# Inverses of two delta rules: half of the heads' Y on the other half of the partitions, products in all four quarters, updates of half the columns

## The chip, the cores and the metric

The kernel runs on one core of a Trainium2 chip, as one program. The metric is the time of one execution on the device in microseconds (us), of which a median of several runs is given. TensorE multiplies, VectorE and ScalarE work on its results in PSUM and on SBUF, GpSimd on SBUF alone, and the DMA queues move data. Each engine runs its own instructions in order; semaphores hold them together.

## What is computed

Two transformer blocks over 1024 tokens of width 1024, one after the other. Each has a mixer with a delta rule. The first block's has 6 heads and two directions, in chunks of 64 tokens:

```python
kb = k * beta[..., None]
a = jnp.where(strict, jnp.einsum('bhnld,bhnsd->bhnls', kb, k) * lmask, 0.0)
t = lax.linalg.triangular_solve(a + eye, jnp.broadcast_to(eye, a.shape),
                                left_side=True, lower=True, unit_diagonal=True)
u = jnp.einsum('bhnls,bhnse->bhnle', t, v * beta[..., None])
wk = jnp.einsum('bhnls,bhnsd->bhnld', t, kb * jnp.exp(gc)[..., None])
```

The second block's has 8 heads and one direction. The reference writes it as a scan over the tokens; the kernel works in chunks of 64 as well and needs the same kind of inverse:

```python
sa = jnp.einsum('bhvk,bhk->bhv', st, a_t)
st = st * w_t[:, :, None, :] + sa[..., None] * b_t[:, :, None, :] + v_t[..., None] * k_t[:, :, None, :]
```

The inverse of each 64x64 triangular matrix is what the change is about. Projections, attention and feed-forward layers take the rest.

## The kernel before

**Units.** 128 tokens are two chunks; chunk c lies on partitions 64c to 64c+63. A unit is the two chunks of all heads of one direction: 16 units of 12 blocks in the first block (`gdn`), 8 units of 16 blocks in the second (`b2`). A block is 64 partitions by 64 columns, block (c, h) at columns 64h. Everything here is float32.

**The inverse.** With M the strict triangle, X starts as the unit matrix minus M's first off-diagonal, and five levels (`LEVELS`, block sizes b = 2, 4, 8, 16, 32) each join pairs of blocks of size b. The kernel holds X both ways round, Xt (turned) and Xa. A level is: Y = the product of M and Xt (`gd_y`, `rw_y`), masked by VectorE to the part that level b fills (lines 1636 and 2950, into Ym); then the products of Xa and Ym (`gd_xt`, `rw_xt`) and of Ym and Xa (`gd_xa`, `rw_xa`); then VectorE subtracts the first from Xt (lines 1642, 2955) and the second from Xa (1644, 2957). The last level makes no Xa. All these products go through `pe_blocks` (matmul at lines 1551 and 2682), which goes through the heads and for each through c = 0 and 1: rows 0 to 63 of the array with output partitions 0 to 63, then rows 64 to 127 with 64 to 127. Ahead of the levels, `gd_t` and `rw_t` (lines 1584, 2885) turn the start by a product with the unit matrix; VectorE adds the unit matrix to give Xt (1632, 2945), and GpSimd adds it to the unturned start for Xa (1687, 2986).

**Other products of 64x64 blocks.** The key products (line 1576, and `pe_features`, line 2695), those of the state (1720, 1734, 3011) and w (1605, 2919) change their row half and output half with every product.

**Order.** Every engine's function is a generator; `together` and `loop` step through them in the same order on every engine. In the first block interval n steps the scan of an earlier pair of units, the second half of unit n-1 and the first half of unit n, and between them the neighbourhood attention (`pe_na` and its companions). In the second, interval i steps the scan of unit i-2 (`pe_scan`), the inverse of unit i-1 (`pe_in`), the preparation of unit i (`pe_pre`) and, at half the pace, the attention `pe_fox`, whose rest follows the loop.

**Banks.** PSUM has 8 banks. `bk.take(key, ring)` gives the next bank of a ring; `bk.pair` is a bank and the one after it. `bk.room` waits until the last holder has been emptied. In the first block `PAIR` is bank 0 (with 1) for kk, w and the scan's products, `ONE_BANK` the ring 2, 3, 4 for everything else. In the second, `PAIR` is bank 0 (with 1) and `ONE_BANK` the ring 2, 3. Attention has its own.

## Time and profile before

| | us |
|---|---|
| median of 3 runs | 4546.52 |
| lowest, highest | 4536.28, 4548.52 |
| the profiled execution | 4550.43 |
| its span | 4549.1 |
| first block's delta rule with neighbourhood attention | 658 to 1071 |
| second block's delta rule with attention | 2761 to about 3334, then attention alone |

The profile is one execution. Busy time counts the time in which an engine has an instruction in work; matmul records overlap, so their durations add up to more. A float32 product of 64x64 blocks appears as two records. PE is the matmul, PEld the weight load, DVE is VectorE, ACT ScalarE, POOL GpSimd; L1551 is a line of the kernel. In the groups, "busy, mean ns | idle before" ends with what ended the idle time.

### The profile page before, as it was taken

To read this page: it belongs to the slowest core of one execution; us is meant where nothing else is said; L and a number is where in the kernel's file an instruction comes from. 1 tells how busy PE (TensorE), PEld (TensorE's weight loads), DVE (VectorE), ACT (ScalarE), POOL (GpSimd) and SP (SyncE) were. 2 spreads that over 40 slices of the span, in tenths; PEclk is the share of its full clock that TensorE was granted. 3 is DMA by queue.
4 is the path that set the end of the run, shared out by engine and by line. 5 is a ranking of instruction groups with operands and counts; after the bars stand their busy time and mean duration, and the time that the engine had idled before them with its cause. 6 is when DMAs were issued, how large, how long until landed. Compare 5 with 4: busy or idle time off the path is not lost. (4 is left out here: it accounts for less than half of the span.)

```text
span 4549.1 us, 75162 instructions
## 1 busy us (share of the span) xinstructions
PE 4046.0 (89%) x33230; PEld 3288.3 (72%) x33230; DVE 2075.1 (46%) x3302; ACT 1251.5 (28%) x1786; POOL 454.3 (10%) x442
## 2 busy tenths in 40 slices
PE   6999849995898899999899996878868989999979
PEld 5788727774676688888588785666656768888867
DVE  4633426554333444445513214655633365655662
ACT  4222244332222221121411214334221232222231
POOL 0001102231201000000200002232201200000010
PEclk9999869997899899999899998998967989999989
DMA  5211120113112111111122323011003211111101
GB/s 180 87 43 62 45 74 6 30 30 139 40 37 93 38 55 47 47 47 55 65 95 89 116 88 90 26 52 44 7 33 137 97 41 52 47 47 47 56 31 63
DMA packets 213687, 281.94 MB, mean 62 GB/s; under 512 B 15580, under 2 KB 170972, under 8 KB 213236
## 3 DMA queue, kind: packets, MB, share of 16 engines
q1 hardware_dynamic: 176048, 185.58, 13.0%
q10 hardware_dynamic: 37316, 91.56, 5.3%
q8 instruction: 263, 4.31, 0.4%
q14 instruction: 60, 0.49, 0.0%
HBM read 217.11 MB, written 60.00 MB: 61 GB/s over the span
## 5 line engine op out<-in xcount | busy, mean ns | idle before, releaser
L425 PE MATMUL ps<-sb_a_h,sb_whi 128*128 128x512 f32 (+1 forms) x3008 | 1206.1, 401 | 128.5 <-DVE sb_a_h L516 66.2
L426 PE MATMUL ps<-sb_a_h,sb_wlo 128*128 128x512 f32 (+1 forms) x3008 | 1192.3, 396 | 0.0
L427 PE MATMUL ps<-sb_a_h,sb_whi 128*128 128x512 f32 (+1 forms) x3008 | 1191.7, 396 | 0.0
L425 PEld LDWEIGHTS ps<-sb_a_h,sb_whi 128*128 128x128 f32 (+1 forms) x3008 | 575.4, 191 | 289.5 <-issue 91.4
L427 PEld LDWEIGHTS ps<-sb_a_h,sb_whi 128*128 128x128 f32 (+1 forms) x3008 | 576.7, 192 | 123.7
L426 PEld LDWEIGHTS ps<-sb_a_h,sb_wlo 128*128 128x128 f32 (+1 forms) x3008 | 578.1, 192 | 118.6 <-issue 1.0
L387 DVE TENSOR_TENSOR sb_wlo<-sb_wraw,sb_whi 128x2048 fp32r<-128x2048 f32 (+3 forms) x146 | 315.8, 2163 | 428.7 <-ACT sb_whi L379 405.0
L1850 DVE TENSOR_TENSOR sb_x<-sb_x,ps 128x512 f32<-128x512 f32 x480 | 314.4, 684 | 299.3 <-PE ps L427 299.1
L379 ACT ACTIVATE sb_whi<-sb_wraw 128x2048 fp32r<-128x2048 f32 (+3 forms) x146 | 260.4, 1784 | 678.1 <-PE ps L427 509.1
L425 PE MATMUL ps<-sb_a_g,sb_whi 128*128 128x512 f32 x896 | 349.7, 390 | 9.6 <-DVE sb_x L1850 9.6
L426 PE MATMUL ps<-sb_a_g,sb_wlo 128*128 128x512 f32 x896 | 348.6, 389 | 0.0
L427 PE MATMUL ps<-sb_a_g,sb_whi 128*128 128x512 f32 x896 | 348.6, 389 | 0.0
L479 POOL TENSOR_TENSOR sb_squares<-sb_squares,sb_a_f 128x512 f32<-128x512 f32 x70 | 88.4, 1275 | 1847.4 <-ACT sb_a_f L471 1846.9
L1551 PEld LDWEIGHTS ps<-sb_b 64*64 64x64 f32 x5760 | 184.6, 136 | 57.7 <-issue 23.6
L1551 PE MATMUL ps<-sb_b 64*64 64x64 f32 x5760 | 200.2, 221 | 21.5 <-DVE sb_b L1644 10.5
L425 PEld LDWEIGHTS ps<-sb_a_g,sb_whi 128*128 128x128 f32 x896 | 168.2, 188 | 48.4 <-DVE sb_x L1850 13.8
L427 PEld LDWEIGHTS ps<-sb_a_g,sb_whi 128*128 128x128 f32 x896 | 168.2, 188 | 35.1
L426 PEld LDWEIGHTS ps<-sb_a_g,sb_wlo 128*128 128x128 f32 x896 | 168.2, 188 | 34.7
L2682 PEld LDWEIGHTS ps<-sb_b 64*64 64x64 f32 x3840 | 133.6, 148 | 64.1 <-DVE sb_b L2957 19.4
L2682 PE MATMUL ps<-sb_b 64*64 64x64 f32 x3840 | 147.2, 234 | 32.1 <-DVE sb_b L2957 11.6
L2096 DVE TENSOR_TENSOR sb_a_f<-sb_a_f 128x512 f32<-128x512 f32 x64 | 44.3, 692 | 185.3 <-ACT sb_a_f L2122 185.3
L513 DVE SCALAR_TENSOR_TENSOR sb_a_f<-sb_x,sb_params,sb_a_f 128x1024 f32<-128x1024 f32 x48 | 83.5, 1763 | 32.2 <-PEq L335 25.0
(467 smaller groups left out, 4980.5 us busy)
## 6 DMA issues: line engine op xcount, KB each, us to landing
sb_wraw<-w_in SPq DMA_DIRECT2D x33, 1024.0 KB, 5.4
sb_wraw<-w_ff SPq DMA_DIRECT2D x32, 1024.0 KB, 5.2
sb_wraw<-w_up SPq DMA_DIRECT2D x22, 1024.0 KB, 5.1
sb_wraw<-w_down SPq DMA_DIRECT2D x11, 1024.0 KB, 4.9
sb_wraw<-w_xkv SPq DMA_DIRECT2D x8, 1024.0 KB, 5.7
sb_wraw<-w_out SPq DMA_DIRECT2D x8, 1024.0 KB, 5.1
sb_a_f<-y ACTq DMA_DIRECT2D x16, 512.0 KB, 5.3
gates<-sb_a_f ACTq DMA_DIRECT2D x32, 256.0 KB, 2.0
```

The lines of the kernel that those rows point to most:

```text
L379: e.activation(WH[j % 2][:, 0:m], WR[j % 2][:, 0:m], ACT.Copy).then_inc(s_whi, 1)
L387: e.tensor_tensor(WL[j % 2][:, 0:m], WR[j % 2][:, 0:m], WH[j % 2][:, 0:m].bitcast(F32), ALU.subtract).then_inc(s_wlo, 1)
L425: e.matmul(o, wh[:, k, c], xh[:, sl], start=(k == 0), stop=False)
L426: e.matmul(o, wl[:, k, c], xh[:, sl], start=False, stop=False)
L427: m = e.matmul(o, wh[:, k, c], xl[:, sl], start=False, stop=(k == t.nk - 1))
L479: e.tensor_tensor(ACC[n % 2], ACC[n % 2], bufs[n % len(bufs)], ALU.add).then_inc(*sa.up())
L513: e.scalar_tensor_tensor(b, xk(k), gain(k), rstd, ALU.mult, ALU.mult).then_inc(*rn.up())
L1551: m = e.matmul(block(ps, c, h), block(lhs, c, h), block(rhs, c, h), start=True, stop=True)
L1850: e.tensor_tensor(o, o, bk[t.key], ALU.add).then_inc(*bk.empty(t.key))
L2096: e.tensor_tensor(b, b, b, ALU.mult).then_inc(*ff_sq.up())
L2682: m = e.matmul(block(ps, c, h), block(lhs, c, h), block(rhs, c, h), start=True, stop=True)
```

## The change

The heads are split into two halves (g = 0 and 1: heads 0 to 2 and 3 to 5, or 0 to 3 and 4 to 7). For the second half Y and Xa lie on the other half of the partitions: the Y of chunk c is written to partitions of chunk 1-c. `quarters()` goes through the products so that successive ones take different quarters of the array; each half of the heads writes a bank of its own, so Y, X and t take pairs, and the first block's rings become pairs 0 and 2 and the single bank 4. Since a level changes only every second run of b columns of X, the products of Xt and Xa stream those 32 columns only (`second`), and VectorE subtracts 192 or 256 columns, not 384 or 512. The Xt and Xa products share one pair (`gd_x`, `rw_x`); the Xa products keep the order of `blocks()`, with outputs in the pair's first bank. The start of Xa for the second half of the heads comes from six (eight) more products with the unit matrix as weights and one more sum on VectorE; GpSimd's sum covers only the first half. The diff, with the second block's part cut to its changed lines (its Y and X products are as in the first, with 4 for 3 heads, 128 for 96 and 256 for 192 columns, `odd` fixed at 1, and its rings unchanged):

```diff
@@ -1514,7 +1514,7 @@
-            PAIR, ONE_BANK = (0,), (2, 3, 4)
+            PAIR, ONE_BANK = (0, 2), (4,)
...
+            def second(ap, b, odd):
+                return ap.rearrange("p (n z b) -> p n z b", z=2, b=b)[:, :, odd]
+
+            def quarter(ps, c, g, q, w):
+                return ps[64 * c:64 * c + 64, g, w * q:w * q + w]
+
+            def small(ap, c, h):
+                return ap[64 * c:64 * c + 64, 32 * h:32 * h + 32]
+
+            def quarters():
+                return [(c, g, q) for q in range(3) for c in range(2) for g in range(2)]
...
-                ps = bk.take(("gd_t", n), ONE_BANK)
+                bk.take(("gd_t", n), PAIR)
+                ps = bk.pair(("gd_t", n))
                 e.wait_ge(*gd_x0[d].at(s))
                 e.wait_ge(*bk.room(("gd_t", n)))
                 for c, h in blocks():
-                    m = e.matmul(block(ps, c, h), block(Xt, c, h), C("eye", 64 * c, 64 * c + 64), start=True, stop=True)
+                    e.matmul(block(ps[:, 0], c, h), block(Xt, c, h), C("eye", 64 * c, 64 * c + 64), start=True, stop=True)
+                for q in range(3):
+                    for c in range(2):
+                        m = e.matmul(block(ps[:, 1], 1 - c, q), C("eye", 64 * c, 64 * c + 64), block(Xt, c, 3 + q), start=True, stop=True)
                 m.then_inc(*bk.fill(("gd_t", n)))
                 yield
-                for lv in range(5):
-                    e.wait_ge(*bk.emptied(("gd_xa", n, lv - 1) if lv else ("gd_t", n)))
-                    pe_blocks(e, ("gd_y", n, lv), ONE_BANK, M, Xt)
+                odd = 1 - d
+                for lv, b in enumerate(LEVELS):
+                    e.wait_ge(*bk.emptied(("gd_x", n, lv - 1) if lv else ("gd_t", n)))
+                    if lv == 0:
+                        e.wait_ge(*gd_xa0[d].at(s))
+                    bk.take(("gd_y", n, lv), PAIR)
+                    ps = bk.pair(("gd_y", n, lv))
+                    e.wait_ge(*bk.room(("gd_y", n, lv)))
+                    for c, g, q in quarters():
+                        m = e.matmul(quarter(ps, 1 - c if g else c, g, q, 64), block(M, c, 3 * g + q), block(Xt, c, 3 * g + q),
+                                     start=True, stop=True)
+                    m.then_inc(*bk.fill(("gd_y", n, lv)))
                     yield
                     e.wait_ge(*bk.emptied(("gd_y", n, lv)))
-                    pe_blocks(e, ("gd_xt", n, lv), ONE_BANK, Xa, Ym)
+                    bk.take(("gd_x", n, lv), PAIR)
+                    ps = bk.pair(("gd_x", n, lv))
+                    e.wait_ge(*bk.room(("gd_x", n, lv)))
+                    for c, g, q in quarters():
+                        o = 1 - c if g else c
+                        m = e.matmul(v3(quarter(ps, c, g, q, 32), b), block(Xa, o, 3 * g + q),
+                                     second(block(Ym, o, 3 * g + q), b, odd), start=True, stop=True)
                     if lv < 4:
-                        pe_blocks(e, ("gd_xa", n, lv), ONE_BANK, Ym, Xa)
-                    yield
-                e.wait_ge(*bk.emptied(("gd_xt", n, 4)))
+                        for c, h in blocks():
+                            m = e.matmul(v3(small(ps[:, 0, 96:288], c, h), b), block(Ym, c, h),
+                                         second(block(Xa, c, h), b, 1 - odd), start=True, stop=True)
+                    m.then_inc(*bk.fill(("gd_x", n, lv)))
+                    yield
+                e.wait_ge(*bk.emptied(("gd_x", n, 4)))
                 e.wait_ge(*gd_kbv.at(n))
                 pe_blocks(e, ("gd_u", n), ONE_BANK, Xt, R(vbs[d], 384))
                 bk.take(("gd_w", n), PAIR)
...
+                pair = bk.pair(("gd_t", n))
                 e.wait_ge(*bk.filled(("gd_t", n)))
                 e.wait_ge(*gd_xa0[d].at(s))
-                e.tensor_tensor(v6(Xt), v6(bk["gd_t", n][:, 0:384]), m6("eye"), ALU.add).then_inc(*bk.empty(("gd_t", n)))
-                yield
+                e.tensor_tensor(v6(Xt), v6(pair[:, 0, 0:384]), m6("eye"), ALU.add).then_inc(*vo.up())
+                e.tensor_tensor(v6(Xa[:, 192:384]), v6(pair[:, 1, 0:192]), b3(C("eye"), 3, 64), ALU.add).then_inc(*bk.empty(("gd_t", n)))
+                yield
+                odd = 1 - d
                 for lv, b in enumerate(LEVELS):
                     e.wait_ge(*bk.filled(("gd_y", n, lv)))
-                    e.tensor_tensor(v6(Ym), v6(bk["gd_y", n, lv][:, 0:384]), m6(f"L{b}" if d else f"LT{b}"),
+                    e.tensor_tensor(gq(Yms[d]), bk.pair(("gd_y", n, lv))[:, :, 0:192].rearrange("p g (q e) -> p g q e", q=3),
+                                    C(f"L{b}" if d else f"LT{b}").unsqueeze(1).unsqueeze(1).to_broadcast([128, 2, 3, 64]),
                                     ALU.mult).then_inc(*bk.empty(("gd_y", n, lv)))
                     yield
-                    e.wait_ge(*bk.filled(("gd_xt", n, lv)))
+                    pair = bk.pair(("gd_x", n, lv))
+                    x = Xt.rearrange("p (g n z b) -> p g n z b", g=2, z=2, b=b)[:, :, :, odd]
+                    e.wait_ge(*bk.filled(("gd_x", n, lv)))
+                    e.tensor_tensor(x, x, pair[:, :, 0:96].rearrange("p g (n b) -> p g n b", b=b),
+                                    ALU.subtract).then_inc(*(vo.up() if lv < 4 else bk.empty(("gd_x", n, lv))))
                     if lv < 4:
-                        e.wait_ge(*bk.filled(("gd_xa", n, lv)))
-                    e.tensor_tensor(Xt, Xt, bk["gd_xt", n, lv][:, 0:384], ALU.subtract).then_inc(*bk.empty(("gd_xt", n, lv)))
-                    if lv < 4:
-                        e.tensor_tensor(Xa, Xa, bk["gd_xa", n, lv][:, 0:384], ALU.subtract).then_inc(*bk.empty(("gd_xa", n, lv)))
+                        x = second(Xa, b, 1 - odd)
+                        e.tensor_tensor(x, x, v3(pair[:, 0, 96:288], b), ALU.subtract).then_inc(*bk.empty(("gd_x", n, lv)))
                     yield
...
                 e.wait_ge(*gd_x0[d].at(s))
-                e.tensor_tensor(v6(R(Xas[d], 384)), m6("eye"), v6(R(Xts[d], 384)), ALU.add).then_inc(*gd_xa0[d].up())
+                e.tensor_tensor(v6(R(Xas[d], 192)), b3(C("eye"), 3, 64), v6(R(Xts[d], 192)), ALU.add).then_inc(*gd_xa0[d].up())
...
@@ -2878,11 +2936,15 @@
-                ps = bk.take(("rw_t", i), ONE_BANK)
+                bk.take(("rw_t", i), PAIR)
+                ps = bk.pair(("rw_t", i))
-                    m = e.matmul(block(ps, c, h), block(R(XT, 512), c, h), C("eye", 64 * c, 64 * c + 64), start=True, stop=True)
+                    e.matmul(block(ps[:, 0], c, h), block(R(XT, 512), c, h), C("eye", 64 * c, 64 * c + 64), start=True, stop=True)
+                for q in range(4):
+                    for c in range(2):
+                        m = e.matmul(block(ps[:, 1], 1 - c, q), C("eye", 64 * c, 64 * c + 64), block(R(XT, 512), c, 4 + q), start=True, stop=True)
...
@@ -2940,21 +3019,25 @@
+                pair = bk.pair(("rw_t", i))
-                e.tensor_tensor(v6(R(XT, 512)), v6(bk["rw_t", i]), m8("eye"), ALU.add).then_inc(*bk.empty(("rw_t", i)))
+                e.tensor_tensor(v6(R(XT, 512)), v6(pair[:, 0]), m8("eye"), ALU.add).then_inc(*vo.up())
+                e.tensor_tensor(v6(R(XA + 256, 256)), v6(pair[:, 1, 0:256]), b3(C("eye"), 4, 64), ALU.add).then_inc(*bk.empty(("rw_t", i)))
-                    e.tensor_tensor(v6(R(Y, 512)), v6(bk["rw_y", i, lv]), m8(f"LT{b}"), ALU.mult).then_inc(*bk.empty(("rw_y", i, lv)))
-                    yield
-                    e.wait_ge(*bk.filled(("rw_xt", i, lv)))
+                    e.tensor_tensor(gq(R(Y, 512)), split(bk.pair(("rw_y", i, lv)), 0), m24(f"LT{b}"), ALU.mult).then_inc(*bk.empty(("rw_y", i, lv)))
+                    yield
+                    pair = bk.pair(("rw_x", i, lv))
+                    x = R(XT, 512).rearrange("p (g n z b) -> p g n z b", g=2, z=2, b=b)[:, :, :, 1]
+                    e.wait_ge(*bk.filled(("rw_x", i, lv)))
+                    e.tensor_tensor(x, x, pair[:, :, 0:128].rearrange("p g (n b) -> p g n b", b=b),
+                                    ALU.subtract).then_inc(*(vo.up() if lv < 4 else bk.empty(("rw_x", i, lv))))
-                        e.wait_ge(*bk.filled(("rw_xa", i, lv)))
-                    e.tensor_tensor(R(XT, 512), R(XT, 512), bk["rw_xt", i, lv], ALU.subtract).then_inc(*bk.empty(("rw_xt", i, lv)))
-                    if lv < 4:
-                        e.tensor_tensor(R(XA, 512), R(XA, 512), bk["rw_xa", i, lv], ALU.subtract).then_inc(*bk.empty(("rw_xa", i, lv)))
+                        x = second(R(XA, 512), b, 0)
+                        e.tensor_tensor(x, x, v3(pair[:, 0, 128:384], b), ALU.subtract).then_inc(*bk.empty(("rw_x", i, lv)))
```

## Rows read from the trace of the kernel before

**Rows 1.** The page's first part: busy time and share of the span
```profile
PE 4046.0 (89%) x33230; PEld 3288.3 (72%) x33230; DVE 2075.1 (46%) x3302; ACT 1251.5 (28%) x1786; POOL 454.3 (10%) x442
```

**Rows 2.** Busy time by stretch, both delta-rule stages; PEclk is granted clock
```profile
658.00:1071.00 413.00, 369.62 (x10380) 312.45 (x10380) 234.09 (x526) 149.13 (x305) 118.63 (x136) 0.98 0.10 26
2750.00:3330.00 580.00, 449.37 (x8288) 367.07 (x8286) 333.26 (x709) 209.27 (x346) 146.03 (x152) 0.90 0.16 46
```

**Rows 3.** Groups by line, first delta-rule stage: busy, mean | idle before
```profile
L1551 PE MATMUL ps<-sb_b 64*64 64x64 f32 x5760 | 200.2, 221 | 21.5 <-DVE sb_b L1644 10.5 <-issue 5.2 <-DVE sb_b L1636 3.4
...
L1642 DVE TENSOR_TENSOR sb_b<-sb_b,ps 128x384 f32<-128x384 f32 x80 | 44.3, 553 | 68.8 <-PE ps L1551 68.1
L1644 DVE TENSOR_TENSOR sb_b<-sb_b,ps 128x384 f32<-128x384 f32 x64 | 35.0, 547 | 0.0
```

**Rows 4.** Order of time, one level of the first unit, alone
```profile
675.10 0.92 PE L1551 MATMUL ps<-sb_b 64*64 64x64 f32 x24 [1.19 <-DVE sb_b L1644]
...
676.67 1.61 PE L1551 MATMUL ps<-sb_b 64*64 64x64 f32 x48 [0.66 <-DVE sb_b L1636]
...
679.48 0.74 PE L1551 MATMUL ps<-sb_b 64*64 64x64 f32 x18 [1.19 <-DVE sb_b L1644]
```

**Rows 5.** Groups by line, second delta-rule stage
```profile
L2682 PE MATMUL ps<-sb_b 64*64 64x64 f32 x3840 | 147.2, 234 | 32.1 <-DVE sb_b L2957 11.6 <-DVE sb_b L2950 9.4 <-DVE sb_b L3099 6.5
...
L2955 DVE TENSOR_TENSOR sb_b<-sb_b,ps 128x512 f32<-128x512 f32 x40 | 27.5, 686 | 57.0 <-PE ps L2682 56.7
...
L2957 DVE TENSOR_TENSOR sb_b<-sb_b,ps 128x512 f32<-128x512 f32 x32 | 21.8, 680 | 0.0
...
L2776 DVE TENSOR_TENSOR sb_b<-sb_b 128x512 f32<-128x512 f32 x8 | 11.2, 1405 | 0.3
...
L3073 DVE TENSOR_TENSOR sb_b<-sb_b,ps 128x256 f32<-128x256 f32 x16 | 6.7, 419 | 12.3 <-PE ps L3027 12.3
```

**Rows 6.** Order of time, second stage: two-quarter and four-quarter products
```profile
3261.28 1.16 PE L2695 MATMUL ps<-sb_b 64*64 64x64 f32 x64
...
3292.34 2.08 PE L2682 MATMUL ps<-sb_b 64*64 64x64 f32 x64
```

**Rows 7.** Order of time, first stage's end: four-quarter product
```profile
1069.04 0.58 PE L1734 MATMUL ps<-sb_x,sb_b 64*64 64x64 f32 x24 [1.25 <-DVE sb_x L1758]
```

**Rows 8.** Order of time, second stage: full-array weights, 64 and 128 columns
```profile
2945.23 1.95 PE L2390 MATMUL ps<-sb_x 128*128 128x64 f32 x16
...
2961.63 1.12 PE L3055 MATMUL ps<-sb_b 128*128 128x128 f32 x8
```

**Rows 9.** Waits, first stage: us in total, times, longest
```profile
PEld ps L1551 <- DVE sb_b L1644: 20.3, 25, 1.4
...
PEld ps L1551 <- DVE sb_b L1636: 9.2, 18, 0.9
```

**Rows 10.** Waits, second stage
```profile
PEld ps L2682 <- DVE sb_b L2957: 19.4, 18, 1.6
...
PEld ps L2682 <- DVE sb_b L2950: 16.4, 17, 2.4
```

**Rows 11.** Line 2682: its engine idle before it until (us, times)
```profile
  DVE sb_b L3099: 13.5, 8
```

**Rows 12.** Order of time, second stage: state product, then the transposing product
```profile
3263.94 1.15 PE L3011 MATMUL ps<-sb_b 64*64 64x64 f32 x32 [1.50 <-DVE sb_b L2941]
...
3265.74 0.69 DVE L3069 TENSOR_TENSOR sb_b<-sb_b,ps 64x512 f32<-64x512 f32 x1
...
3266.08 1.15 PE L2885 MATMUL ps<-sb_consts,sb_b 64*64 64x64 f32 x32
```

**Rows 13.** Busy time by stretch inside the second stage
```profile
2800.00:2850.00 50.00, 38.28 (x826) 30.53 (x825) 29.37 (x65) 17.69 (x35) 16.94 (x19) 0.97 0.12 30
...
3000.00:3050.00 50.00, 37.89 (x554) 29.90 (x554) 27.35 (x63) 17.84 (x34) 15.33 (x15) 0.83 0.08 23
...
3300.00:3350.00 50.00, 28.51 (x392) 22.74 (x386) 16.64 (x28) 17.14 (x20) 2.71 (x4) 0.77 0.20 68
```

More of the change, by code:

```diff
@@ L1652, in ac_prep @@
                 if n >= 2:
-                    e.wait_ge(*bk.emptied(("gd_xt", n - 2, 4)))
+                    e.wait_ge(*bk.emptied(("gd_x", n - 2, 4)))
                 if s >= 2:
@@ L2675, in block, with second, quarter, small @@
                 return ap[64 * c:64 * c + 64, 64 * h:64 * h + 64]
+            def second(ap, b, odd):
+                return ap.rearrange("p (n z b) -> p n z b", z=2, b=b)[:, :, odd]
+            def quarter(ps, c, g, q, w):
+                return ps[64 * c:64 * c + 64, g, w * q:w * q + w]
+            def small(ap, c, h):
+                return ap[64 * c:64 * c + 64, 32 * h:32 * h + 32]
+            def quarters():
+                return [(c, g, q) for q in range(4) for c in range(2) for g in range(2)]
             def pe_blocks(e, key, lhs, rhs):
@@ L2898, in pe_in @@
                     yield
-                for lv in range(5):
-                    e.wait_ge(*bk.emptied(("rw_xa", i, lv - 1) if lv else ("rw_t", i)))
-                    pe_blocks(e, ("rw_y", i, lv), R(M, 512), R(XT, 512))
+                for lv, b in enumerate(LEVELS):
+                    e.wait_ge(*bk.emptied(("rw_x", i, lv - 1) if lv else ("rw_t", i)))
+                    if lv == 0:
+                        e.wait_ge(*rw_xa0.at(i))
+                    bk.take(("rw_y", i, lv), PAIR)
+                    ps = bk.pair(("rw_y", i, lv))
+                    e.wait_ge(*bk.room(("rw_y", i, lv)))
+                    for c, g, q in quarters():
+                        m = e.matmul(quarter(ps, 1 - c if g else c, g, q, 64), block(R(M, 512), c, 4 * g + q),
+                                     block(R(XT, 512), c, 4 * g + q), start=True, stop=True)
+                    m.then_inc(*bk.fill(("rw_y", i, lv)))
                     yield
                     e.wait_ge(*bk.emptied(("rw_y", i, lv)))
-                    pe_blocks(e, ("rw_xt", i, lv), R(XA, 512), R(Y, 512))
+                    bk.take(("rw_x", i, lv), PAIR)
+                    ps = bk.pair(("rw_x", i, lv))
+                    e.wait_ge(*bk.room(("rw_x", i, lv)))
+                    for c, g, q in quarters():
+                        o = 1 - c if g else c
+                        m = e.matmul(v3(quarter(ps, c, g, q, 32), b), block(R(XA, 512), o, 4 * g + q),
+                                     second(block(R(Y, 512), o, 4 * g + q), b, 1), start=True, stop=True)
                     if lv < 4:
-                        pe_blocks(e, ("rw_xa", i, lv), R(Y, 512), R(XA, 512))
+                        for c, h in blocks():
+                            m = e.matmul(v3(small(ps[:, 0, 128:384], c, h), b), block(R(Y, 512), c, h),
+                                         second(block(R(XA, 512), c, h), b, 0), start=True, stop=True)
+                    m.then_inc(*bk.fill(("rw_x", i, lv)))
                     yield
-                e.wait_ge(*bk.emptied(("rw_xt", i, 4)))
+                e.wait_ge(*bk.emptied(("rw_x", i, 4)))
                 e.wait_ge(*bk.emptied(("rw_g", i)))
```

2 lines of the change are left out of this document (1 added, 1 removed).

## The prediction

> **What bounds the kernel now.** I read the page's first part, then busy time by stretch, then the groups and waits of the two stages, then the order of time. The page says that TensorE is busy for 89% of the span and VectorE for 46% [rows 1]. The change touches only two stages: the first block's delta rule (413 us) and the second block's (580 us, of which the last part is attention alone). In the first TensorE is busy 369.6 us of 413 (0.895), in the second 449.4 of 580 (0.775); VectorE has 234 and 333 us [rows 2]. So nothing outside these 993 us can move, and inside them TensorE comes first.
>
> Busy TensorE is not all of it. The inverses are a ping-pong: a product of TensorE, an update of VectorE, a product. The order of time shows one level of the first unit with nothing beside it: the Y product starts at 675.10, the products of Xt and Xa take 1.61 us from 676.67, and the next level's Y product starts at 679.48, released by the update of line 1644, 4.38 us after the last [rows 4]. In the steady state other units, attention and the scan fill the gaps: the idle time of the matmuls of line 1551 is 21.5 us in all, and of line 2682 it is 32.1 [rows 3, 5]. The weight loads, which start first, wait for the update of Xa (lines 1644 and 2957) 25 times for 20.3 us, and 18 times for 19.4 us [rows 9, 10]. So I take TensorE's issue as the bound for most of both stages, and VectorE's updates as a part of the path where those waits stand.
>
> **TensorE, what is saved.** A float32 product of 64x64 blocks is two records (5760 records for the first stage's 16 units of 180 products). All products of a level now go in a diagonal order: two quarters of the array. For 64 such records the trace has 2.08 us; taking 0.22 us as the length of a single record (mean 221 ns, rows 3), (2.08 - 0.22)/63 = 29.5 ns a record. The products of line 2695 change their quarter with every product and use all four: 64 records take 1.16 us, 14.9 ns a record [rows 3, 6]. The first stage has the same pair: 48 records in 1.61 us, 29.6 ns, against 24 in 0.58 us, 15.7 ns [rows 4, 7]. So four quarters halve the spacing, by 14.6 ns a record. The changed Y and Xt products use all four.
>
> First stage, a unit: 5 Y batches and 5 Xt batches of 24 records, 240 x 14.6 ns = 3.5 us saved. The turned Xa of the second half of the heads comes from 6 more products (12 records, two quarters, 0.35 us). Net 3.15 us, times 16 units = 50.4 us. Second stage, a unit: 10 batches of 32 records, 4.67 us, less 16 records more, 0.47 us: 4.2 us, times 8 = 33.6 us.
>
> **Half the columns.** Xt's and Xa's products now stream 32 columns, not 64. No row shows a product of 32. The nearest is the step from 128 to 64 columns with weights of 128 columns: 8 records of 128 columns take 1.12 us (140 ns each with the tail), 16 records of 64 columns 1.95 us (122 ns each) [rows 8]. Half the columns gave 13%, not half. The weights keep their 64 columns in this change, and I take the same to hold: nothing gained. The bounds are no gain and half the spacing; half would save 5 x 24 x 7.5 ns + 4 x 24 x 14.8 ns = 2.3 us a unit in the first stage and 3.1 in the second, with the shares of use below 33 + 19 = 52 us.
>
> The Trainium skill, TensorE: Matmul & The Clock Gate, section LDWEIGHTS (loading the stationary operand), states that a load takes its columns over 1.2 GHz whatever its rows; by that rule a 64-column load is an estimated 53 ns in each quarter, and a narrower stream behind it gains nothing. The trace agrees: full-array records of 64 columns are spaced 122 ns or less, near the load of 128 columns that the rule puts at 107.
>
> **VectorE.** 512 columns take 686 ns and 256 take 419 [rows 5]: 1.04 ns a column. In the first stage each update loses 192 of 384 columns, 0.20 us; nine a unit make 1.80, and the added sum with the unit matrix on the other half costs 0.547 - 0.20 = 0.35 us. That is 1.45 x 16 = 23 us of busy time. In the second stage 9 x 0.267 - 0.42 = 1.98 us, times 8 = 16 us. Only what TensorE waits for counts: 25 waits x 0.40 us (two updates) = 10 and 18 x 0.53 = 9.6 us [rows 9, 10], less the added sum at the same shares of use (16 x 0.35 x 25/64 + 8 x 0.42 x 18/32 = 4.1 us). That is 15.5 us. The Y mask keeps its 384 or 512 columns. Its wait is the smaller one (9.2 and 16.4 us) and stays.
>
> The updates now touch runs of 2, 4, 8, 16 and 32 columns. No row has such runs. Lower bound: no cost. Upper bound: the slowest float32 rate in the stage, 1405 ns for 512 columns, 2.74 ns a column [rows 5]; then 192 columns take 0.67 and 256 take 0.85 us, and the updates get 0.12 and 0.17 us longer instead of shorter. I take no cost, since what slows that row is no property that its shape shows, and 686 ns is the rate of every update out of PSUM here.
>
> The Trainium skill, Vector Engine (DVE) Microarchitecture Reference, section 5.2 Measured stream behaviour on trn2, states that runs of two adjacent aligned words stream at the full rate; by it the sum stands as it is. No run here shows it yet.
>
> **How much of TensorE's saving arrives.** In slices where TensorE waits anyway, shorter products only lengthen the wait. I take the busy shares of the stages: 50.4 x 0.895 = 45.1 and 33.6 x 0.775 = 26.0, together 71.1 us.
>
> **Waits that move.** In the first stage the rings change from one pair and three banks to two pairs and one bank. A fill waits for the fill two before it. Following the order, those are nearly always the unit's own dependence (Y before X before Y); the key product kk and the scan's second product wait for less. The lone bank holds only decays, u and outputs, each emptied some rounds before. I count nothing, covered by that distance; without it each of about 16 intervals would pay one VectorE step of 0.55 us, 9 us. In the second stage t, Y and X leave banks 2 and 3 for the only pair, which the state product uses. There t now waits until VectorE has emptied that product: the second of its two operations starts at 3265.74 and ends at 3266.43, while t issues at 3266.08 [rows 12]. That is 0.4 us where an attention step stands between them, up to 1.4 where none does (the product starts at 3263.94 and lasts 1.15); behind t queue the g and kv products and VectorE's masks. 7 units x 1.0 = 7 us lost. Against it, products no longer wait for banks that output work holds: 13.5 us of idle in 8 waits on line 3099 [rows 11], of which I take half, since the same VectorE operation still stands ahead of the consumer in its queue. The two cancel. GpSimd's sum is halved and its end was not the last thing waited for; TensorE's new wait for it is met already by VectorE's. Nothing.
>
> **Sum.** 71.1 + 15.5 = 87 us. The profiled execution took 4550.4 us (span 4549.1), 3.9 above the median of 4546.5. 4550.4 - 87 = 4463.8, less 3.9: **4460 us**, 1.9% faster.
>
> **Rivals.**
> Narrow products do run in half the time. For it: 140 to 122 ns is for full-width weights, and quarter products are only bounded together. Against it: the 13%. It gives 4460 - 52 = 4408. Chance 0.12.
> Short runs slow VectorE to the upper bound: 43 waits get 0.25 to 0.33 us longer where I had them shorter, 12 us lost for 20 gained: 4492. Chance 0.08.
> Four quarters do not overlap. In the rows of four quarters each row half of the array writes a bank of its own; in the change both row halves write into each bank, on different partitions. Then only the 9 us of added products and VectorE's 15.5 us are left: about 4540, within 0.3%. Against it: the diagonal order also puts both halves in one bank, and each quarter's spacing is the same there (2 x 29.5) as with four (4 x 14.9). Chance 0.05.
> The Trainium skill, TensorEngine Tiling (Array Packing), section Gotcha 1: PSUM Pressure, says that different row tiles cannot access the same PSUM bank simultaneously; this is the rule that speaks for that rival. The two-quarter rows speak against it as far as different partitions go.
> The clock decides, and the kernel is slower. With less work between the same waits TensorE's granted clock may fall (a mean over its two levels, 2.4 GHz as 1.00 and 1.2 GHz as 0.50). It is 0.98 and 0.90 over the two stages [rows 2], and inside the second 0.97 where TensorE is busy 38.28 of 50 us, but 0.83 at 37.89 and 0.77 at 28.51 [rows 13]. At 0.83 in both stages the cost is 369.6 x (0.98/0.83 - 1) + 449.4 x (0.90/0.83 - 1) = 67 + 38 = 105 us, more than the 87: 4550.4 + 18 - 3.9 = 4565 us, slower by 0.4%. It decides from a granted clock of 0.846 in both; at that point gain and loss are equal. Against it: four quarters at once keep the array at least as full while it works, and the first stage stands near 1.00. Chance 0.05.
> That the saving is mostly off the path (half arrives): 4503. Chance 0.07.
>
> **How the numbers follow.** The forecast's own case has 0.63, with 4435 to 4485 for the choice of shares. The range 4400 to 4525 takes in the narrow, the short-run and the half case and leaves out the bank and the clock case and small tails. A change under 0.3% (14 us) can't be told from none. Faster by more: 0.90; within: 0.05; slower: 0.05.
>
> **What would show it.** In the profile after: 24 records of the Y product in about 0.58 us and 32 in 0.70, the X products (48) in about 1.27 us and (64) in 1.65, updates of 192 columns at 0.35 us and of 256 at 0.42, the first unit's level at about 3.3 us from 4.38, TensorE busy some 50 and 34 us less, clocks near 0.98 and 0.90. X products of 0.8 us would mean that narrow ones are cheap; Y products still at 0.92 that the quarters don't overlap; updates of 0.55 that runs cost. New waits of t for line 3069 above 1.5 us, or of X for another unit's bank, would make me wrong from the other side.

## The result and the profile after

The changed kernel took 4516.12 us in the median of five runs (4504.9 to 4522.52) beside 4548.17 us for the kernel before on the same chip: ratio 0.9929 [0.9907, 0.995], 32 us saved. The forecast was 87 us (4460), so the direction was right, and the time lies inside the range of 4400 to 4525, but the gain is little over a third of the one forecast. The profiled span went from 4549.1 to 4516.8 us. Ratios in this document are formed from fast executions alone; one of the six of the fastest version below took 9364 us at a granted clock of 0.46, and it is in that version's median but not in its ratio. The page's first part of the changed kernel, to be read beside [rows 1]:

```profile
PE 4021.2 (89%) x33550; PEld 3259.4 (72%) x33550; DVE 2032.3 (45%) x3326; ACT 1251.2 (28%) x1786; POOL 446.0 (10%) x442
```

VectorE lost 43 us of busy time; TensorE lost only 25, where 84 were to go. The two stages, by busy time in the stretch of each (columns as in [rows 2]: PE, PEld, DVE, ACT, POOL, granted clock):

```profile
663.00:1045.00 382.00, 334.30 (x10572) 277.48 (x10572) 208.03 (x540) 148.57 (x304) 112.10 (x136) 0.93 0.10 28
2732.00:3301.00 569.00, 451.47 (x8395) 364.76 (x8396) 318.29 (x719) 208.38 (x344) 145.37 (x155) 0.79 0.16 46
```

From its first decay product to its last output sum the first stage took 412.3 us before and 382.0 after. The second, from GpSimd's first fill of a tile to the last output sum, took 572.9 and 568.3. By those marks TensorE was busy for 369 us at a clock of 0.98 and for 445 at 0.89 before. So the first stage gave 30 us and the second 5. Each length is of one execution, and stages of the same code differ between executions by about as much as the second gave: the second stage of the kernel before took 572.9 and 569.2 us in two profiles, the changed one 563.7, 568.3 and 572.6 in three, and the changed first stage 381.8 to 388.6 in five. In the second TensorE is busy for longer than before, 451 against 445 us, although its products stand closer together, at a clock of 0.79. Busy time times the mean clock of the stretch gives an estimate of the work at full clock: 369 x 0.98 = 362 before, 334 x 0.93 = 311 after, 51 less; 445 x 0.89 = 396 and 451 x 0.79 = 356, 40 less. The forecast had 50.4 and 33.6. The work fell about as computed. How much the clock took back is what the experiments below ask.

The lengths of the parts are as forecast where they can be seen alone at full clock. The order of time at the end of the first stage:

```profile
1026.85 0.58 PE L1615 MATMUL ps<-sb_b 64*64 64x64 f32 x24 [0.71 <-DVE sb_b L1687]
1027.36 0.66 PE L1253 MATMUL ps<-sb_consts,sb_b 128*128 128x128 f32 x4
1028.11 0.55 PE L1625 MATMUL ps<-sb_b 64*64 64x32 f32 x24
1028.48 0.88 PE L1629 MATMUL ps<-sb_b 64*64 64x32 f32 x24
1030.07 0.58 PE L1615 MATMUL ps<-sb_b 64*64 64x64 f32 x24 [0.71 <-DVE sb_b L1687]
```

A Y batch (line 1615) takes 0.58 us, the narrow Xt batch (1625) 0.55, the narrow Xa batch in two quarters (1629) 0.88, and a level 1030.07 - 1026.85 = 3.22 us. The sign that the prediction named, the first unit's level, did not come: it takes 678.09 - 673.64 = 4.45 us, no less than the 4.38 before, and its Y batch 0.92 us. That 0.92 was to mean that the quarters don't overlap. It means half clock instead, by the slice of 10 us that it lies in:

```profile
673.64 0.92 PE L1615 MATMUL ps<-sb_b 64*64 64x64 f32 x24 [0.93 <-DVE sb_b L1671]
678.09 0.92 PE L1615 MATMUL ps<-sb_b 64*64 64x64 f32 x24 [0.71 <-DVE sb_b L1687]
```
```profile
670.00:680.00 10.00, 6.12 (x144) 5.42 (x148) 3.39 (x8) 0.00 (x0) 2.97 (x4) 0.50 0.42 111
```

VectorE's groups in that stage, mask, Xt and Xa, and its Xt update in the second (columns as in [rows 3]):

```profile
L1676 DVE TENSOR_TENSOR sb_b<-ps,sb_consts 128x384 f32<-128x384 f32 x80 | 44.0, 553 | 34.0 <-PE ps L1615 33.5
L1683 DVE TENSOR_TENSOR sb_b<-sb_b,ps 128x192 f32<-128x192 f32 x80 | 28.1, 352 | 45.3 <-PE ps L1629 43.0 <-PE ps L1625 2.1
L1687 DVE TENSOR_TENSOR sb_b<-sb_b,ps 128x192 f32<-128x192 f32 x64 | 22.2, 347 | 0.0
```
```profile
L3036 DVE TENSOR_TENSOR sb_b<-sb_b,ps 128x256 f32<-128x256 f32 x40 | 16.7, 418 | 40.9 <-PE ps L2983 33.6 <-PE ps L2979 7.1
```

Short runs cost nothing: the 80 Xt updates of the first stage take 332 to 356 ns each, 2-column runs among them, and those of the second 418 on average, where whole ones of 256 columns took 419. Where the clock falls is seen in slices of 10 us. Two neighbouring ones of the changed kernel's second stage:

```profile
2850.00:2860.00 10.00, 5.75 (x53) 4.60 (x52) 4.23 (x8) 9.85 (x18) 0.80 (x2) 0.53 0.01 2
2860.00:2870.00 10.00, 9.92 (x88) 7.21 (x87) 3.95 (x9) 1.19 (x2) 7.25 (x6) 0.50 0.01 2
```

In the first TensorE is busy for 5.75 of 10 us. Attention waits there until ScalarE and VectorE have copied its transposes out of PSUM (lines 2493 and 2472):

```profile
PE ps L2421 <- ACT sb_x L2493: 2.3, 1, 2.3
PE ps L2433 <- DVE sb_x L2472: 1.6, 1, 1.6
```

In the second it is busy throughout, with 88 records, at half clock. Over the whole stage the largest wait of attention is that of its transposes for ScalarE's exponentials (lines 2485 and, before, 2442), after and before:

```profile
PE ps L2421 <- ACT sb_x L2485: 15.1, 16, 3.5
```
```profile
PE ps L2378 <- ACT sb_x L2442: 14.8, 12, 2.8
```

So the kernel before has the same waits, but 4 of the 57 slices of its second stage stand at 0.55 or less; after, 10 of 56.

### The profile page after: what moved, and what is told of

Its sections match the earlier page's. It is cut to its first block and busy times, and to the rows that moved or that the text cites. A ratio compares the mean times of both kernels' runs of the same rounds, so it can differ in the third digit from the quotient of the medians.

```text
span 4516.8 us, 75730 instructions
## 1 busy us (share of the span) xinstructions
PE 4021.2 (89%) x33550; PEld 3259.4 (72%) x33550; DVE 2032.3 (45%) x3326; ACT 1251.2 (28%) x1786; POOL 446.0 (10%) x442
## 5 line engine op out<-in xcount | busy, mean ns | idle before, releaser
L2165 ACT ACTIVATE sb_a_f<-ps 128x512 f32<-128x512 f32 x64 | 38.3, 598 | 215.0 <-PE ps L427 215.0
L471 ACT ACTIVATE sb_a_f<-sb_x 128x512 f32<-128x512 f32 x70 | 44.1, 632 | 184.3 <-DVE sb_x L1893 184.3
L3431 ACT ACTIVATE sb_a_f<-ps 128x512 f32<-128x512 f32 x88 | 52.6, 598 | 151.2 <-PE ps L427 151.2
L2433 PE MATMUL ps<-sb_x 128*128 128x64 f32 x432 | 75.2, 345 | 3.1 <-DVE sb_x L2472 2.3
```

What stands on the lines that cost most here:

```text
L471: e.activation(bufs[(n - 2) % len(bufs)] if n >= 2 else ACC[n], xk(t.f)[:, t.hf * 512:(t.hf + 1) * 512], ACT.Square).then_inc(*sq.up())
L2433: m = e.matmul(bk["fx_y", p, qb // 4][:, c:c + 64], lg_of(p, qb, g)[:, j * 128:(j + 1) * 128], R(VF + j * 128 + g * 64, 64), start=(j == 0 ...
L3431: e.activation(raws[i % 3][:, 2:514], bk[t.key], ACT.Copy).then_inc(*bk.empty(t.key))
```

## The experiments

Times are medians, with the ratio to the kernel before run on the same chips beside them. Stage lengths and stage clocks are by the marks above, from each one's profiled execution; the ratios carry more weight than they do.

**Each stage alone, wide Xt products, another order.** The first two kernels have the change in one stage only. The other two are the changed kernel with one edit each:

```
# wide_xt, both stages; Xt's update reads the used columns out of the 64
-  m = e.matmul(v3(quarter(ps, c, g, q, 32), b), block(Xa, ..), second(block(Ym, ..), b, odd), ..)
+  m = e.matmul(quarter(ps, c, g, q, 64), block(Xa, ..), block(Ym, ..), ..)
# two_quarters, both stages: all products of one pair of quarters, then all of the other
-  return [(c, g, q) for q in range(3) for c in range(2) for g in range(2)]
+  return [(c, g, q) for g in range(2) for q in range(3) for c in range(2)]
```

First stage alone, expected:

> The change in the first block's delta rule alone; the second block's stage is as before. The clock theory (the stages save what the record counts say, and a lower granted clock takes part of it back): the first stage is about 30 us shorter as in the changed kernel, the second stage keeps its 573 us and its granted clock of 0.90, total about 4517 us. The rival, that the whole change cost the second stage something through its waits and the first something through its own, expects the same first stage but cannot tell from this run why. If the two stages add up, this run and the next one give ratios whose distances from 1 sum to 0.7%.

Second stage alone, expected:

> The change in the second block's delta rule alone. Both theories: about 4543 us, 5 us below before, since its stage went from 573 to 568 us. The clock theory expects the second stage's granted clock near 0.78 as in the changed kernel, although the first stage stays at 0.98; the wait theory expects new long waits of the t, Y and X products for the pair of banks, several us a unit, and no dependence on the clock.

Wide Xt, expected:

> The changed kernel, but the Xt products stream all 64 columns again (four quarters, VectorE still updates only half of the columns; the Xa products stay at 32). Clock theory in the form that narrow streams leave the array emptier at the same spacing: batches of 24 records still take 0.55 to 0.58 us, and the granted clock rises in both stages, by a third to a half of what was lost (0.90 towards 0.94, 0.78 towards 0.84), total 4485 to 4505 us. Rival: only the share of time in which TensorE works counts for the clock; then clock and time stay within 8 us of the changed kernel. A second rival: 64 columns cost time after all and the kernel gets slower by up to 20 us.

Two quarters at a time, expected:

> The changed kernel, but quarters() goes through one half of the heads after the other, so that successive products alternate between two quarters only; widths, placement, banks and updates are those of the changed kernel. By the forecast's terms it gives back 240 records x 14.6 ns a unit in the first stage (56 us in all, 0.895 of it on the path: 50) and 10 x 0.47 us x 8 = 37 us in the second (29 on the path): 4595 us if the clock stays. If the clock theory in the form of busy share holds, TensorE is busy longer per product and the granted clock returns towards 0.98 and 0.90, so that less than half of that is lost: 4530 to 4560 us. If the array's filling counts instead, the clock falls further and it is above 4595 us.

Measured: first stage alone 4515.0 us (0.9912 [0.9886, 0.9937]), second alone 4544.61 (0.9982 [0.9967, 0.9998]); second-stage clocks 0.90 and 0.79. Both as expected: the first stage carries the gain, and the second's clock falls by that stage's own change. The two gains add up to 1.1%, where 0.7% was expected if the stages add up; the intervals leave that open. Wide Xt: 4514.35 (0.9913 [0.9897, 0.9929]), clocks 0.94 and 0.81: no gain that can be told. My theory had 4485 to 4505; the time is the first rival's. Two quarters: 4514.33 (0.9914 [0.9895, 0.9932]), against all that was expected. Its second stage:

```profile
L2969 PE MATMUL ps<-sb_b 64*64 64x64 f32 x1280 | 48.3, 257 | 5.2 <-DVE sb_b L3040 4.8
L2979 PE MATMUL ps<-sb_b 64*64 64x32 f32 x1280 | 43.5, 241 | 9.0 <-DVE sb_b L3031 9.0
```

The same two lines in the changed kernel:

```profile
L2969 PE MATMUL ps<-sb_b 64*64 64x64 f32 x1280 | 36.0, 266 | 4.9 <-DVE sb_b L3040 4.8
L2979 PE MATMUL ps<-sb_b 64*64 64x32 f32 x1280 | 34.2, 254 | 10.3 <-DVE sb_b L3031 10.2
```

The order costs 91.8 - 70.2 = 21.6 us of busy time on these lines, yet the stage is no longer (562.9 us against 568.3): the clock came to 0.82, attention's lines took less (line 2433 44.7 us against 49.5), and all of TensorE's busy time there is 450 against 451 us. In work at full clock it is 91.8 x 0.82 - 70.2 x 0.79 = 20 us, not the 37 of 80 batches of 32 records at 14.6 ns: a batch whose first half uses one pair of quarters and whose second half the other is already part of the way.

**Idle products, short updates.** Four products of the unit matrix with itself were put ahead of the wait for the exponentials, in all 32 blocks of attention, once in each kernel; they write the bank that the transposes overwrite:

```
+  e.wait_ge(*bk.room(key))
   if a == 0:
+      for _ in range(4 if g == 0 else 0):
+          e.matmul(ps[:, 0:128], C("ident"), C("ident"), start=True, stop=True)
       e.wait_ge(*fx_exp[g].at(8 * p + qb))
-  e.wait_ge(*bk.room(key))
```

In the changed kernel, expected:

> The changed kernel with four idle products more (identity by identity, 128 columns, written into the bank that the next transposes overwrite) in each of the attention's 32 query blocks, put ahead of the wait for ScalarE's exponentials, where TensorE stands idle for 91 us in all in the profile of the changed kernel. Nothing computed changes. Theory (the granted clock of the second stage, 0.79, follows from TensorE's idle stretches and costs the second stage's gain): the clock comes to 0.87 or more, and the time to 4470 to 4500. Rival (the clock is not tied to these gaps, or the lower clock costs nothing): clock 0.77 to 0.83 and 4512 to 4535, since 32 times some 0.66 us is added and partly hidden.

In the kernel before, expected:

> The kernel before with the same four idle products in each of the 32 query blocks. Theory: its second stage has a granted clock of 0.89 and comes to 0.94 or more; TensorE's 445 us there shrink by some 25 us, of which about 0.78 count: 4525 to 4535. Rival (fillers are only a cost): 4548 to 4565.

The other two kernels take the updates apart: the kernel before with narrow products and half updates, and the changed kernel with Xt's update whole.

```
# halves_only, on the kernel before, and the same for Xa and the second stage
-  m = e.matmul(block(ps, c, h), block(lhs, c, h), block(rhs, c, h), ..)
+  m = e.matmul(v3(ps[64*c:64*c+64, 32*h:32*h+32], b), block(lhs, c, h), second(block(rhs, c, h), b, odd), ..)
-  e.tensor_tensor(Xt, Xt, bk["gd_xt", n, lv][:, 0:384], ALU.subtract)
+  x = second(Xt, b, 1 - d)
+  e.tensor_tensor(x, x, v3(bk["gd_xt", n, lv][:, 0:192], b), ALU.subtract)
```

> The kernel before, in which the Xt and Xa products give the 32 columns of each block that are used and VectorE's updates take 192 (256) columns instead of 384 (512); heads, banks and order of products stay as they were. By the prediction's terms only VectorE's part (15.5 us on the path) is left: 4533, ratio 0.9966. Rival (the saving of the whole change comes from the short updates, as the run with two quarters, which lost nothing, suggests): 4510 to 4525, ratio 0.992 to 0.995. The last case: no gain, 4548, if VectorE's time lies beside TensorE's.

Xt's update whole, expected:

> The changed kernel with the Xt products 64 columns wide and Xt's update over all 384 (512) columns again; Xa's stays half. If the short updates lie on the path, 5 levels of 16 units lose 0.2 us each and 5 of 8 units 0.21 us: 16 + 8 us by their duration, so 4530 to 4540. If they lie beside TensorE's work: 4510 to 4520, as the run with wide products alone.

Measured: fillers in the changed kernel 4507.78 (0.9908 [0.9877, 0.9939]), in the kernel before 4537.51 (0.9968 [0.9953, 0.9983]). Their second stages have clocks of 0.83 and 0.92 but lengths of 575.3 and 573.1 us, so nothing was won there. In the changed kernel the theory's 0.87 and its time were missed, and the time lies between it and the rival; in the kernel before the time is 3 us above the theory's 4525 to 4535, and the clock 0.92 where 0.94 was expected. What was won lies behind the stage, where attention runs alone: from the second stage's end to the kernel's end 1216 us became 1196, and 1215 became 1198.

Xt's update whole: 4511.54 (0.9919 [0.9888, 0.995]), the second case of its expectation: beside 0.9913 with the short update no cost can be told. In the profiles the first stage is longer, 391.2 against 382.8 us with the same wide products, which is little outside what equal stages differ by, and the second is not (560.0 against 561.5).

The surprise was the kernel before with narrow products and short updates: 4576.17 us, slower than before, ratio 1.0057 [1.0039, 1.0076], which none of its three cases had. It has less VectorE work and as many records as the kernel before. Its stages:

```profile
664.00:1079.00 415.00, 380.01 (x10375) 323.82 (x10370) 206.39 (x524) 148.76 (x304) 118.78 (x136) 0.94 0.09 25
2770.00:3377.00 607.00, 493.63 (x8266) 406.94 (x8267) 316.86 (x711) 208.57 (x344) 148.85 (x155) 0.80 0.15 44
```

The work at full clock is unchanged (493.6 x 0.80 = 395 against 396 us), the clock fell from 0.89 to 0.80, and the second stage became 33 us longer. This is the slowest of its seven executions (4588.7 us), so the lengths overstate it.

**Which half lowers the clock, and where fillers pay.** The first kernel keeps the short updates and gives the products their 64 columns back; the second has five idle products in the last pair's eight blocks only; the third adds full-width Xt products and updates in the second stage.

```
# half_wide, on the kernel before
+  e.tensor_tensor(x, x, second(bk["gd_xt", n, lv][:, 0:384], b, 1 - d), ALU.subtract)
# fill_tail
+      for _ in range(5 if p == 3 and g == 0 else 0):
```

> The kernel before with VectorE's half updates alone: all products stay 64 columns wide and in their banks, and the updates read and write every other group of b columns, 192 (256) elements a partition. The run with narrow products and the same half updates took 4576, with a granted clock of 0.80 in its second stage against 0.89. Theory A (narrow products lower the clock, since they feed the array less): here the clock stays at 0.88 to 0.90 and the time is 4530 to 4548. Theory B (the shorter updates move the queues against one another, whatever the products' width): the clock is again 0.78 to 0.82 and the time 4565 to 4585.

Fillers in the last eight blocks, expected:

> The changed kernel with five idle products (ten records) in each of the last pair of heads' eight attention blocks alone, the 100 us behind the second stage, which ran at a granted clock of 0.50 to 0.53 in both kernels. The run with fillers in all 32 blocks had 0.67 to 0.84 there. Theory (those 100 us are 20 us shorter at the higher clock, and the fillers in the other 24 blocks cost some 7 us): 4490 to 4500, the clock of the second stage 0.79 as in the changed kernel. Rival (the gain of that run came from the second stage): 4512 to 4520.

The two together, expected:

> As the run before it, and in the second stage the Xt products and Xt's update over the full width, whose own run had 560 us there against 568. The first stage is that of the changed kernel (382 us; 391 with the full update). If the stages add up: 4480 to 4490. If the 8 us of the second stage were chance: 4490 to 4500.

Short updates with wide products: 4537.07 us, 0.9979 [0.9964, 0.9995]. Its stages:

```profile
662.00:1072.00 410.00, 372.71 (x10380) 315.88 (x10380) 206.63 (x525) 148.63 (x305) 118.65 (x136) 0.97 0.10 26
2762.00:3328.00 566.00, 444.92 (x8266) 362.62 (x8267) 316.53 (x711) 208.31 (x344) 147.69 (x155) 0.89 0.16 47
```

The same number of records, the same VectorE time (316.5 against 316.9 us in the second stage); what differs is the columns that Xt's and Xa's products stream, 64 against 32, and with them whether VectorE reads every other run of b columns or packed ones. The clock is 0.89 against 0.80. The medians are 39 us apart on different chips; by the ratios, 0.9979 and 1.0057, it is 0.8% or 35 us. Three of its 56 slices stand at 0.55 or less, against 15 of 60. Nor does the clock hang on the one profile: over a whole execution it is 0.912 to 0.919 in all seven of the narrow version and 0.925 to 0.931 in all ten of the wide one, with 0.924 to 0.932 in the kernel before. Theory A held.

Fillers in the last eight blocks: 4504.07 (0.9903 [0.9886, 0.992]), 12 us under the changed kernel by medians and ratios, though the intervals overlap, with the second stage's clock still 0.79. The stretch behind the second stage, first of the changed kernel, then with fillers:

```profile
3300.00:3350.00 50.00, 30.25 (x96) 18.53 (x94) 11.75 (x46) 17.95 (x32) 4.20 (x10) 0.58 0.03 11
3350.00:3400.00 50.00, 41.10 (x146) 29.49 (x145) 12.60 (x57) 11.69 (x23) 2.68 (x6) 0.52 0.00 1
```
```profile
3312.00:3362.00 50.00, 34.56 (x157) 23.61 (x155) 13.62 (x55) 20.50 (x38) 5.40 (x13) 0.75 0.03 11
3362.00:3402.00 40.00, 34.25 (x201) 26.08 (x202) 12.33 (x50) 9.51 (x18) 1.79 (x4) 0.87 0.00 0
```

The median is between theory and rival. From the second stage's end to the kernel's end its profile has 1195 us; that stretch takes 1195 to 1198 us in all five versions with fillers and 1207 to 1216 in the ten without. So the gain comes from those blocks, and the 20 us that I had read from one pair of profiles were the upper end of 10 to 21. The two together took 4492.28 us (0.9886 [0.9862, 0.991]), the second case of its expectation; its interval overlaps that of the fillers alone, and the profiled execution was the slowest of six (4518.79), with 579.6 us in the second stage. Whether full-width Xt products help there stays unclear.

**Wide products inside the change.** Each product streams its whole block again, used columns on one side and unused ones on the other, and the next block's product writes over the unused ones. So the used columns lie packed as in the changed kernel, and nothing of VectorE's work moves. For that the heads are gone through backwards where the used columns stand on the far side (not shown in the excerpt below).

```
+  def whole(e, out, at, p, s, lhs, rhs, b, z):
+      at += 32 * s - 32 * z
+      return e.matmul(out[64*p:64*p+64, at:at+64].rearrange("p (z n b) -> p z n b", z=2, b=b), lhs,
+                      rhs.rearrange("p (n z b) -> p z n b", z=2, b=b), start=True, stop=True)
-  m = e.matmul(v3(quarter(ps, c, g, q, 32), b), block(Xa, ..), second(block(Ym, ..), b, odd), ..)
+  m = whole(e, ps[:, g], 32, c, q, block(Xa, ..), block(Ym, ..), b, odd)
```

> The changed kernel with every Xt and Xa product streaming all 64 columns again: the 32 unused ones of a block are written over the next block's place and overwritten by its product, so that the used ones stay packed and VectorE's short updates stay as they are. Products, their order, records and banks are those of the changed kernel. In the kernel before, the same step (half updates with wide instead of narrow products) took the second stage's clock from 0.80 to 0.89 and the time from 4576 to 4537. Theory (the narrow products are what lowers the clock): clock 0.96 and 0.87 or more; the first stage's 311 us of full-clock work cost 13 us less and the second's 356 us 46 us less, of which 0.9 and 0.78 count: 12 + 36 us, so 4465 to 4480. Rival (the clock falls since the four-quarter order leaves the array idle for longer, whatever the width, as the run with wide Xt products alone suggests, 0.94 and 0.81): 4508 to 4520.

With the fillers of the last eight blocks as well, expected:

> The run before it with the five idle products in each of the last pair's eight attention blocks, which were worth 12 us by the medians (4504 against 4516) on the changed kernel. Theory: 12 us under the run with wide products alone, 4453 to 4468. If the wide products bring nothing: 4498 to 4508.

Measured: 4498.5 us (0.988 [0.9867, 0.9893]) and 4481.82 us (0.9846 [0.9834, 0.9859]). The stages with wide products, without fillers, in the fastest of its four executions (4491.34 us):

```profile
663.00:1040.00 377.00, 327.98 (x10572) 271.80 (x10572) 208.11 (x541) 148.57 (x304) 112.14 (x136) 0.96 0.10 28
2733.00:3279.00 546.00, 410.95 (x8394) 333.35 (x8395) 318.70 (x718) 208.14 (x344) 145.06 (x154) 0.87 0.17 48
```

The clocks are the theory's, 0.96 and 0.87; two of 54 slices of the second stage are at 0.55 or less. Over whole executions the clock is 0.919 to 0.923 in all four, and 0.909 to 0.914 in the five of the changed kernel. TensorE's busy time fell by 40 us in the second stage against the changed kernel, with the same count of records, and the stage by 22 us (568.3 to 546.5); the first by 5 (382.0 to 376.6). The time lies between theory (4465 to 4480) and rival (4508 to 4520): the mechanism holds, and the share of it that arrives was set too high. At full clock the wide Xt and Xa batches together take 1.27 us, the narrow ones 1029.36 - 1028.11 = 1.25. With fillers it is 17 us less, on the same chip and with intervals apart, where 12 were expected; the time is above the 4453 to 4468 of its theory, since the run under it was. Its stages, whose code is that of the run without fillers but for the place of one wait and the idle products in the last blocks, took 377.6 and 555.0 us at 0.95 and 0.85, so the 546.5 is at the short end. It is the fastest version measured: 70 us under the kernel before and, by the ratios, 38 under the changed one.

## Why the prediction came out as it did

**What bounds the kernel.** Nothing moved outside the two stages (3564 us outside them before, 3567 after), as forecast. That TensorE's issue is the bound for most of both is true only in part: from the changed kernel to the one with wide products its busy time in the two stages falls by 6.3 + 40.5 = 47 us, and the time by 22 (by the ratios) to 27 (by the stages' lengths), about half.

**TensorE, what is saved** was right: 51 and 40 us of work at full clock against 50.4 and 33.6, batches of 0.58 us. The rival that quarters do not overlap fell. The Trainium skill, TensorEngine Tiling (Array Packing), section Gotcha 1: PSUM Pressure, says that different row tiles cannot access a bank at once; here both row halves write each bank of a pair, on different partitions, and the 24 records take 0.58 us, so the trace does not bear it out in that form.

**Half the columns, "nothing gained"** was right for the records' length ((0.88 - 0.22)/23 = 28.7 ns a record in two quarters, against 29.5 with 64 columns) and is the first of two steps that failed. "Nothing gained" was entered as nothing changed, and a price below nothing was not bounded. Narrow products lowered the granted clock. In the old layout they cost 35 us by the ratios 1.0057 and 0.9979; inside the change, by 0.9929 and 0.988, 0.5% or 22 us of the 55 missing.

**How much arrives** is the second, and the larger one. With wide products, which cost 0.02 us a level at full clock, and clocks of 0.96 and 0.87 the change brings 1.2% or 55 us, not 87. The shares of 0.895 and 0.775, taken from the busy share of whole stages, are one term of the 32 us left, and VectorE's 15.5 another; the residue of the clock below is the third. No run parts the three. There is a trap in the numbers: put into the sum with those shares, the clocks 0.93 and 0.79 alone give (311/0.93 - 311/0.98) x 0.895 + (356/0.79 - 356/0.89) x 0.775 = 15 + 39 = 54 us, nearly the whole 55. The version with wide products shows that this is chance: giving most of the clock back returned 22 us.

**The clock rival** was named with a chance of 0.05 and a break-even of 0.846 in both stages. Measured were 0.93 and 0.79. Its mechanism was the right one, its reason ("less work between the same waits") only part of it: with wide products and just as few records the clocks are 0.96 and 0.87. My argument against it, that four quarters keep the array full, did not look at what each record streams. What is left of it, 0.96 against 0.98 and 0.87 against 0.89, is worth 328.0 - 315/0.98 = 6.6 and 411.0 - 358/0.89 = 8.8 us of busy time.

**VectorE, 15.5 us on the path.** Its durations were right (352, 418 ns), the share on the path was too large. Alone in the kernel before, without the added sum, the short updates bring 0.2% or 10 us (2 to 16 by the interval), where the same working gives 19.6; in the changed kernel a whole Xt update costs nothing that can be told. In the version with wide products the two stages are 35.7 and 26.4 us shorter than before, 62 together, in its fastest execution, and with the fillers 34.7 and 17.9, 53 together: either is less than the 71.1 of TensorE's term alone. TensorE's idle time went from 43 to 49 us and from 128 to 136 instead of falling.

**Waits that move.** The turned product waits for the state product's second operation as forecast, 6.9 us in 6 waits, against 7 us; the longest, 1.6, is at the 1.5 that was named as the limit:

```profile
PE ps L2944 <- DVE sb_b L3152: 6.9, 6, 1.6
```

No wait for another unit's bank is among the first. The relief on output's banks can't be told apart from the rest.

**The range** held the time by luck: it reached up to 4525 for the case that half the gain arrives off the path (4503), and a little over a third arrived, in part through the clock, whose case the range was to leave out. Narrow products at half the time (4408) and slow short runs (4492) both fell.

**What stays open.** Wide Xt products alone, five of a unit's nine batches of narrow products, gave back 0.01 and 0.02 of the clock; Xt's and Xa's together 0.03 and 0.08. Why it is so uneven no run tells, nor what part of the order in four quarters has in the clock; two quarters at a time gave 0.94 and 0.82 with narrow products. Nor was it tried whether a narrower Y would matter, or fillers placed inside the stages at other waits.

## What to carry to other kernels

Where TensorE is the bound and its granted clock is not at 1.00 before, work out a change in work at full clock (busy time times granted clock) and forecast the clock as a term of its own, with a price on both sides. What arrives of a saving in busy time was here about half, not the stage's busy share; bound that share too. Columns that are streamed for nothing are not free to take away: if a record is not shorter for it, keep the full width, and pack the results by letting the next product overwrite the unused ones. In a stretch where TensorE waits often and runs at half clock, a few idle products ahead of the wait can pay; where it has other work, they only fill it.

## What the hardware showed that was not expected

- Products of 64x64 weights that stream 32 columns instead of 64 take nearly as long (28.7 ns a record against 29.5) and lowered the granted clock: 0.80 against 0.89 over stages of 607 and 566 us, with as many records and equal work of the other engines.
- An order that uses one pair of quarters for the first half of a batch and the other pair for the second half takes 0.74 us for 24 records at full clock, between 0.58 for four quarters in turn and the 0.88 of one pair (narrow products).
- Ten idle records ahead of each of eight waits brought a stretch of 100 us from a clock of 0.52 to 0.58 up to 0.75 to 0.87, and made the kernel 12 us shorter in one version and 17 in another.
- VectorE updates in runs of 2 to 32 float32 columns in SBUF keep the rate of whole ones (192 columns 352 ns, 256 columns 418), and so do those that read such runs out of PSUM as well (353 and 421 ns, short updates with wide products in the kernel before). The Trainium skill, Vector Engine (DVE) Microarchitecture Reference, section 5.2 Measured stream behaviour on trn2, states as much for runs of two aligned words in SBUF, and the trace agrees.
